# Two transformer blocks: level products of both directions in one, and experts gathered in pairs

## The reference, cut to what matters

```python
b = jnp.cumsum(gc.astype(jnp.float32), axis=2)
diff = jnp.where(lower_tri, b[:, :, :, None, :] - b[:, :, None, :, :], -jnp.inf)
a = jnp.einsum('bhtk,bhsk,bhtsk->bhts', qc, kc, jnp.exp(diff))
o = (jnp.einsum('bhts,bhsv->bhtv', a, vc)
     + jnp.einsum('bhtk,bhkv->bhtv', qc * jnp.exp(b), state))
...
# gla_bidir: for d in range(2), d == 1 with every sequence flipped; the outputs are summed
...
# moe_swiglu
top_v, top_i = lax.top_k(logits, TOP_K)
top_w = jax.nn.softmax(top_v, axis=-1)
gates = jnp.sum(jax.nn.one_hot(top_i, N_EXPERTS, dtype=jnp.float32) * top_w[..., None], axis=-2)
for e in range(N_EXPERTS):
    y = y + gates[..., e:e + 1] * swiglu_2(h, w_gate[e], w_up[e], w_down[e]).astype(jnp.float32)
```

## Time and profile before

| | |
|---|---|
| median of 3 runs | 3079.16 us (3079.08 to 3087.44) |
| the profiled execution | 3083.53 us, of which its span is 3081.6 us |
| mean granted TensorE clock | 0.924 of full speed |
| busy share of the span | TensorE 87%, VectorE 60%, ScalarE 49% |
| bytes read | 558.28 MB, 182 GB/s over the span |
| both level stages | 76.65 us and 45.90 us |
| eight experts | 104.5 us each but the first |

### The profile page before, as it was taken

How to read it: one execution, slowest core, us unless ns; L and a number is a source line. 1 busy time by engine, 2 the same in 40 slices (tenths; PEclk the granted TensorE clock), 3 DMA queues, 4 the chain that set the end, 5 groups by cost and what they waited for, 6 DMA issues and landing times.

```text
span 3081.6 us, 44103 instructions
## 1 busy us (share of the span) xinstructions
PE 2680.0 (87%) x17684; PEld 2350.5 (76%) x17684; DVE 1842.1 (60%) x2603; ACT 1498.9 (49%) x1927; POOL 11.1 (0%) x53
## 2 busy tenths in 40 slices
PE   5987668999989666998878999968899999999997
PEld 3865447999979455997857998947778787878786
DVE  3246734545542564544855554845588888888886
ACT  4224234434442425434454444454467666666665
POOL 0000000000000000000000000000000000000000
PEclk7998878999989877998889999979999999999998
DMA  6250302444533141553412454403388888888884
GB/s 265 83 214 33 137 25 99 178 178 180 187 112 137 69 164 55 179 189 125 151 39 99 151 180 151 177 8 116 116 321 340 323 339 336 332 316 336 337 333 186
DMA packets 80210, 562.10 MB, mean 182 GB/s; under 512 B 8705, under 2 KB 12033, under 8 KB 12434
## 3 DMA queue, kind: packets, MB, share of 16 engines
q1 hardware_dynamic: 79746, 558.32, 48.1%
q0 software_dynamic: 272, 1.05, 0.1%
HBM read 558.28 MB, written 1.05 MB: 182 GB/s over the span
## 4 chain that ended last, share of the span: by engine, by line
PE 77%; DVE 10%; ACT 7%; issue 3%; DMA 0%; DVEq 0%; ACTq 0%; SPq 0%; PEldq 0%; PEld 0%
PE psum L229 76%; ACT ring_hi L220 1%; DVE ring_lo L223 1%; DVE hT L599 1%; DVE Z L1256 1%; DVE hT L372 1%; PE psum L522 1%; ACT hT L358 1%; PE psum L1579 1%; ACT hT L563 1%; DVE Z L1011 1%; DVE Z L1032 1%; ACT a_hi L361 1%; DVE Z L1012 0%; ACT L353 0%
## 5 line engine op out<-in xcount | busy, mean ns | idle before, releaser
L223 DVE TENSOR_TENSOR ring_lo<-ring,ring_hi 128x2048 fp32r<-128x2048 f32 x479 | 1097.1, 2292 | 510.3 <-ACT ring_hi L220 507.4
L220 ACT ACTIVATE ring_hi<-ring 128x2048 fp32r<-128x2048 f32 x479 | 916.0, 1914 | 509.2 <-PE psum L229 508.6
L229 PE MATMUL psum<-a_hi,ring_hi 128*128 128x256 f32 (+1 forms) x2448 | 742.0, 303 | 107.4 <-DVE h_lo L366 50.4
L229 PE MATMUL psum<-a_hi,ring_lo 128*128 128x256 f32 (+1 forms) x2448 | 732.4, 299 | 0.0
L229 PE MATMUL psum<-h_lo,ring_hi 128*128 128x256 f32 (+1 forms) x2128 | 633.8, 298 | 0.0
L229 PEld LDWEIGHTS psum<-a_hi,ring_hi 128*128 128x128 f32 x2448 | 480.5, 196 | 133.4 <-issue 86.7
L229 PE MATMUL psum<-ring_hi,a_hi 128*128 128x512 f32 (+2 forms) x1744 | 538.0, 374 | 6.2 <-DVE h_lo L366 4.0
L229 PEld LDWEIGHTS psum<-a_hi,ring_lo 128*128 128x128 f32 x2448 | 481.8, 197 | 10.4
L229 PEld LDWEIGHTS psum<-h_lo,ring_hi 128*128 128x128 f32 x2128 | 419.7, 197 | 7.5
L229 PE MATMUL psum<-ring_lo,a_hi 128*128 128x512 f32 (+2 forms) x1040 | 371.1, 357 | 0.0
L229 PEld LDWEIGHTS psum<-ring_hi,a_hi 128*128 128x128 f32 x1744 | 325.0, 189 | 58.4 <-issue 4.4
(11 more groups left out here) (222 smaller groups left out, 2529.5 us busy)
## 6 DMA issues: line engine op xcount, KB each, us to landing
ring<-in_stream SPq DMA_DIRECT2D x527, 1024.0 KB, 4.8
cst<-in_constants SPq DMA_DIRECT2D x1, 1216.0 KB
xT<-in_xT SPq DMA_DIRECT2D x1, 1024.0 KB, 9.6
xT<-in_ctxT SPq DMA_DIRECT2D x1, 1024.0 KB, 11.9
xT<-in_memT POOLq DMA_DIRECT2D x1, 1024.0 KB, 8.6
out_y<-hT SPq DMA_DIRECT2D x1, 1024.0 KB, 4.8
Z<-in_level_masks SPq DMA_DIRECT2D x1, 896.0 KB
vec<-in_vectors SPq DMA_DIRECT2D x1, 225.0 KB, 11.0
```

Source lines behind the costliest of these rows:

```text
L220: e.activation(hi, raw, ACT.Copy).then_inc(sem("piece_rounded"), 1)
L223: e.tensor_tensor(lo, raw, hi.bitcast(F32), ALU.subtract).then_inc(sem("piece_split"), 1)
L229: ins = pe.matmul(*args, **kw)
```

## The change

It does four things. (1) One step per level: both directions' decays are formed by instructions over both channel halves (512 columns in layer 0, 256 in layer 1), keys and queries are scaled into two buffers, and one product keys x queries holds one direction above and the other below the diagonal; one mask takes both. Two mod pieces follow a level. VectorE now waits for its own scaling before it overwrites the exponentials. (2) The gather is done for two experts at once: 256 columns in float32r, with the tokens held as a rounded and a rest part (`g_tok`, written by ScalarE and VectorE in the router), so 32 products per pair. Only every second expert has one. (3) The last `turn` of an expert stands behind the first down piece, and the split of one down piece is moved ahead of the last hidden tile on both engines. (4) The scatter is done in two halves, after rounds 2 and 3. The mask table and its load are half as large.

```diff
-            for i, (l, d) in enumerate(gla_steps()):
+            for l in range(LEVELS):
                 await_next(pe, "level")
                 for t in tiles:
                     if t == 3:
-                        pe.wait_ge(sem("gram_read"), rd + (i + 1) * nt + 1)
+                        pe.wait_ge(sem("gram_read"), rd + (l + 1) * nt + 1)
                     else:
-                        pe.wait_ge(sem("gram_read"), rd + i * nt + (nt if t == 0 else t + 1))
+                        pe.wait_ge(sem("gram_read"), rd + l * nt + (nt if t == 0 else t + 1))
                     for h in range(4):
                         r = slice((h % 2) * HD, (h % 2 + 1) * HD)
-                        m = gM[i % 2][r, h // 2, t * P:(t + 1) * P]
-                        mm(pe, gram(t, h), m, m, start=True, stop=True,
+                        at = slice(t * P, (t + 1) * P)
+                        mm(pe, gram(t, h), keys_at[r, h // 2, at], queries_at[r, h // 2, at], start=True, stop=True,
                            last_of="grams" if h == 3 else None)
-                if i < len(IN_LEVELS[layer]):
-                    pe_mod_piece(pe, IN_LEVELS[layer][i])
+                for m in in_level(layer, l):
+                    pe_mod_piece(pe, m)
...
+            def decay(l):
+
                 h = 1 << l
+                for d in range(2):
+                    lo, hi = gla_level(l, gB[d], n)
+                    e_lo, e_hi = gla_level(l, gE[d], n)
+                    m = lo[:, :, :, h - 1:h] if d == 0 else hi[:, :, :, 0:1]
+                    mb = m.to_broadcast([P, 2, n // (2 * h), h])
+                    a, b, ea, eb = (hi, lo, e_hi, e_lo) if d == 0 else (lo, hi, e_lo, e_hi)
+                    dve.tensor_tensor(ea, a, mb, ALU.subtract)
+                    dve.tensor_tensor(eb, mb, b, ALU.subtract).then_inc(sem("level_decay"), 1)
+
+            def scaled(l):
+
+                q, k, keys, queries = (gla_level(l, x, n) for x in (GQ, GK, keys_at, queries_at))
+                e = [gla_level(l, gE[d], n) for d in range(2)]
+                await_next(dve, "level_exp", 2)
+                for half in range(2):
+                    dve.tensor_tensor(keys[half], k[half], e[half][half], ALU.mult)
+                    ins = dve.tensor_tensor(queries[half], q[half], e[1 - half][half], ALU.mult)
                 ins.then_inc(sem("level"), 1)
 
...
-            for i, (l, d) in enumerate(steps):
-                scaled(i)
-                if i + 1 < len(steps):
-                    decay(i + 1)
-                mask = lvl_mask[:, 2 * l + d, :].unsqueeze(1).unsqueeze(1).to_broadcast([P, 2, 2, P])
+            for l in range(LEVELS):
+                scaled(l)
+                await_next(dve, "level")
+                if l + 1 < LEVELS:
+                    decay(l + 1)
+                mask = lvl_mask[:, l, :].unsqueeze(1).unsqueeze(1).to_broadcast([P, 2, 2, P])
                 for t in range(nt):
-                    dve.wait_ge(sem("grams"), gr + nt * (i + 1) + t + 1)
-                    dve.wait_ge(sem("gram_read"), own + nt * i + t + 1)
+                    dve.wait_ge(sem("grams"), gr + nt * (l + 1) + t + 1)
+                    dve.wait_ge(sem("gram_read"), own + nt * l + t + 1)
                     dve.copy_predicated(by_bank(t), mask, grams(t))\
...
-                    dve.tensor_copy(h_tok[:, t, d * 512:(d + 1) * 512], bank[4 + 2 * t + d][:, :])
+                    await_next(dve, "turned_rounded")
+                    at = slice(d * 512, (d + 1) * 512)
...
+            for t in range(2):
+                for d in range(2):
+                    await_next(act, "h_turned")
+                    act.activation(g_tok[t][:, d * 512:(d + 1) * 512], bank[4 + 2 * t + d][:, :], ACT.Copy)\
+                       .then_inc(sem("turned_rounded"), 1)
...
+        def pe_gather(pe, pre, r, pair):
 
             pe.wait_ge(sem(pre + "_selected"), r + 1)
-            for k in range(KT):
+            for k in range(KT if pair else 0):
                 for t in range(2):
-                    mm(pe, bank[6 + k // 4][:, (k % 4) * P:(k % 4 + 1) * P], h_tok[:, t, k * P:(k + 1) * P],
-                       select[:, t, :], start=t == 0, stop=t == 1,
-                       last_of=pre + "_gathered" if k == KT - 1 and t == 1 else None)
+                    mm(pe, g_sums[k // 4][:, k % 4 * T:(k % 4 + 1) * T], g_tok[t][:, k * P:(k + 1) * P],
+                       select[:, t, :, :].rearrange("p u n -> p (u n)"), start=t == 0, stop=False)
+                for t in range(2):
+                    mm(pe, g_sums[k // 4][:, k % 4 * T:(k % 4 + 1) * T], g_tok[2 + t][:, k * P:(k + 1) * P],
+                       select[:, t, :, :].rearrange("p u n -> p (u n)"), start=False, stop=t == 1,
+                       last_of=pre + "_gathered" if k % 4 == 3 and t == 1 else None)
...
+        def act_gather(act, pre, r, i, pair):
+            if pair is not None:
+                for half in range(2):
+                    act.wait_ge(sem(pre + "_gathered"), pair * 2 + half + 1)
+                    act.activation(g_part[0][:, half * 1024:(half + 1) * 1024], g_sums[half], ACT.Copy)\
+                       .then_inc(sem(pre + "_slots_rounded"), 1)
...
+                pos = POS[:, t, following[0]]
+                ins = dve.tensor_scalar(select_w[:, t, :], const("iota"), pos, GT[:, t, following[0]],
                                         ALU.is_equal, ALU.mult)
+                for u in range(2 if pair else 0):
+                    ins = dve.tensor_scalar(select[:, t, u, :], const("iota"), POS[:, t, following[u]], None,
+                                            ALU.is_equal)
...
-                if j == 2:
-                    pe_scatter(pe, pre, r, i)
-            turn(PAIRS - 1)
+                if j in (2, 3):
+                    pe_scatter(pe, pre, r, i, (2 * j - 4, 2 * j - 3))
             for q in range(2 * FT):
...
+                if q == 3:
+                    turn(PAIRS - 1)
                 if q == FT + 1:
                     pe.wait_ge(sem(pre + "_x_added"), r * 4 + 4)
-                    pe_gather(pe, pre, r + 1)
-
-        def act_expert(act, pre, r, i, it):
+                    pe_gather(pe, pre, r + 1, i == 1)
...
+                else:
+                    split_ahead(act, "act", it=it)
...
+                if j in (2, 3):
+                    dve_add_scattered(dve, pre, r, (2 * j - 4, 2 * j - 3))
             for j in range(PAIRS):
-                split_ahead(dve, "dve", it=it)
-                if j == 0:
-                    dve_select(dve, pre, r + 1, following)
-                if j == PAIRS // 2 + 1:
-                    dve_gather(dve, pre, r + 1)
+                if j:
+                    split_ahead(dve, "dve", it=it)
+                else:
+                    dve_select(dve, pre, following, i == 1)
+                if j == PAIRS // 2 + 1 and i == 1:
+                    dve_gather(dve, pre, pair + 1)
```

More of the change, by code:

```diff
@@ L932, in by_bank, with in_level @@
             return gA[:, t].rearrange("p (v u) n -> p u v n", v=2)
-        def gla_steps():
-            return [(l, d) for l in range(LEVELS) for d in range(2)]
+        def in_level(layer, l):
+            return IN_LEVELS[layer][2 * l:2 * l + 2]
         def pe_gla_levels(pe, layer):
@@ L969, in act_gla_levels @@
             n = 2 * T if layer == 0 else T
[L970 to L977, removed]
+            for l in range(LEVELS):
+                for d in range(2):
+                    await_next(act, "level_decay")
+                    e = gE[d][:, :, 0:n]
+                    act.activation(e, e, ACT.Exp).then_inc(sem("level_exp"), 1)
+                for m in in_level(layer, l - 1) if l else ():
+                    act_mod_rows(act, m, batch(layer)[0], rows_a)
+            for m in in_level(layer, LEVELS - 1):
+                act_mod_rows(act, m, batch(layer)[0], rows_a)
             phase_end(act)
@@ L982, in dve_gla_levels @@
             nt = n // P
-            steps = gla_steps()
-            def decay(i):
-                l, d = steps[i]
+            def decay(l):
                 h = 1 << l
[L989 to L992, removed]
-                    mb = m[:, c].to_broadcast([P, n // (2 * h), h])
-                    a, b = (hi, lo) if d == 0 else (lo, hi)
-                    ea, eb = (e_hi, e_lo) if d == 0 else (e_lo, e_hi)
-                    dve.tensor_tensor(ea[:, c], a[:, c], mb, ALU.subtract)
-                    ins = dve.tensor_tensor(eb[:, c], mb, b[:, c], ALU.subtract)
-                ins.then_inc(sem("level_decay"), 1)
@@ L1518, in build, with pe_scatter @@
         PAIRS = FT // 2
-        def pe_scatter(pe, pre, s, i):
+        def pe_scatter(pe, pre, s, i, blocks):
             pe.wait_ge(sem(pre + "_y_copied"), s * 2 + 2)
-            for b in range(4):
+            for b in blocks:
                 if b >= 2:
@@ L1529, in pe_scatter, with dve_add_scattered @@
                        start=True, stop=True, last_of=pre + "_scattered" if c == 1 else None)
```

(21 more changed lines are left out.)

90 lines of the change are left out of this document (35 added, 55 removed).

## The result

The changed kernel takes 2992.22 us, the median of four runs (2987.19 to 2995.16), against 3079.62 for the kernel before in the same session (four runs). The ratio is 0.971, with a 95% interval from 0.969 to 0.973: 87 us faster, where 70 were forecast. The profiled execution took 2990.49 us, 93.0 less than that of before.

The account below looks back on a forecast made before the run. VectorE was taken to bound the levels and TensorE the experts. Levels and mask cast 32.8 us plus experts 37.2 made 70.0 saved, from a median of 3079.2 to 3009 us; own range 2999 to 3024, wide range 2992 to 3038.

Parts of the forecast that it names:

- The scatter: In each expert, TensorE's 1.21 us idle mid-scatter would vanish with two blocks in each of two rounds: 9.7 us saved.
- The turning: Before each expert's last hidden-tile turning, TensorE's 2.01 us idle would be filled by four down blocks: 16.1 us saved.
- The gather: Token gather for two experts at once, 32 float32r products of 256 columns in 3.84 us: 13.4 us saved in the loop.
- the late split: Behind the last turning, the fourth down piece's split comes some 0.3 us late in every second expert: 1.2 us lost.
- The levels: Merged level steps: 7.4 us per level in layer 0, 4.1 in layer 1; 19.9 and 12.4 us saved.
- the 0.3 taken off for TensorE's start: Layer 1's levels: 0.3 us deducted from 12.7 saved, because TensorE's first products came at half speed.
- The columns: Modulation columns behind the levels in both layers: no saving in the main forecast, 0 us.
- The transfers bind: Experts' pieces come no faster than 336 GB/s, so only the levels pay: 3046 us; chance 0.06.
- The clock falls in the levels: TensorE, less busy in the level stages, loses clock: price 10 to 19 us, 3019 to 3028; chance 0.12.
- Its opposite: TensorE's clock stays up for the 48 records behind the levels in both layers: 8 us more gained, 3001; chance 0.1.
- The split pieces come late: At four reordered expert places TensorE waits for VectorE's splits: 18 us each per expert; chance 0.07 one or two, 0.03 four.
- The change does nothing: Across the whole kernel, what is removed was already hidden, so the time stays 3079 us; chance 0.02.

Follow-up runs that it names:

- the changed kernel's repeat: The changed kernel timed again without any edit, in the third experiment session beside three variants: 2993.07 us, 0.971 of the kernel before.

## Why the prediction was right or wrong

The mechanisms were right, each where it was said to be. The saving was mis-sized by 17 to 23 us, in these terms.

**The scatter: 1.21 us forecast per expert, 1.67 measured.** The bracket is only the idle time of the one wait; start to start the scatter went from 4.75 to 3.08 us (16 records of 0.19). 8 times the difference is 3.7 us; putting the scatter back costs 12.9 in all.

**The turning: 2.01 forecast, 2.24 measured**, for the same reason: the wait has 0.2 us of its own around the bracket. 1.8 us.

**The gather was right.** 3.84 us per pair as forecast, against 2 x 3.57, or 13.2 us for four pairs, with 12.7 measured alone. So was the late split: in the second expert of a pair VectorE's six comparisons put the split of the fourth down piece so that one product begins 0.44 us after another instead of 0.23: 0.2 us late, where the forecast had 0.3. TensorE, there, in the changed kernel:

```profile
2541.66 0.39 PE L229 MATMUL psum<-ring_lo,Zr 128*128 128x512 f32 x1
2542.10 0.72 PE L229 MATMUL psum<-ring_hi,Zr 128*128 128x512 f32 x2
```

Experts in one sum: 17.9 (turning), 13.3 (scatter), 13.2 (gather), 8.0 (clock) are 52.4; products that take 91.6 us per expert instead of 91.2 in one without a fall give back 3. Half of that is a price of the second scatter round that the forecast didn't have: the product behind a round takes 0.42 us instead of 0.23, start to start. The late split is 0.1 per expert. The profile says 49.4.

**The levels: 32.3 us forecast, 36.0 profiled.** Periods of 7.40 and 4.05 us were forecast as 7.4 and 4.1. In layer 0 VectorE's busy time fell by 20.9, 1 us more than seven times the period's saving. In layer 1 the 0.3 taken off for TensorE's start didn't come: VectorE's idle time in the stage fell from 2.98 to 1.30 us.

**The columns: 0 forecast, 5.9 profiled, of which only some 3 belong to the change.** The wait behind unchanged levels was 9.60, 9.60, 9.60, 6.80, 6.80 and 6.67 us in layer 0 in six profiled executions, and 11.6 to 13.0 in layer 1; behind merged levels 4.97, 4.98, 6.18, 6.52, 6.80 and 7.08 in six (the seventh, with split instructions, had 9.60), and 10.5 to 11.2. The means differ by 2.1 and 1.3. The profiled execution of before was on the high side in both. The difference is the granted clock, 0.50 and 0.90 in the groups of layer 0 of the kernel before and of the changed kernel's repeat:

```profile
361.60:372.00 10.40, 10.40 (x50) 10.31 (x48) 0.73 (x1) 0.00 (x0) 0.00 (x0) 0.50 0.00 0
339.77:345.83 6.06, 6.06 (x50) 5.98 (x48) 1.13 (x2) 0.00 (x0) 0.00 (x0) 0.90 0.44 170
```

That the columns' time turns on the clock was said; that it differs by 3 us between executions of equal work was not.

**Rivals.** *The transfers bind*: false. The three whole pairs drew 352 to 353 GB/s, more than the 336 that an expert had shown, and no wait for a transfer stands in them. By the 358 GB/s per core of the Trainium skill (DMA: Bandwidth & Descriptors, Where 436 GB/s comes from) a pair of two times 33 pieces could not be under some 193 us, an estimate; 196.8 us come near that and decide nothing about it. *The clock falls in the levels*: it was 0.91 in layer 0, down from 0.96, and 0.89 again in layer 1, but the periods stood at VectorE's time, so in the levels themselves it cost nothing that shows. *Its opposite*, columns at full clock with 8 us more: half right in the profile, 3 us by all executions. *The split pieces come late*: only as forecast, 0.2 us a pair. The turning moved without its splits shows that this rival had a real price, all of the turning's gain. *The change does nothing*: false.

## What to carry to other kernels

An idle time on TensorE is worth more than its bracket: measure it start to start, and look whether the products behind it run at half clock, in every repetition of the loop and not in one, since only some showed it here. When a step moves past another, what other engines do ahead for it has to move too, or the wait reappears at the next product with nothing gained. Work which nobody waits for until the end of a stage (columns here) is cheaper in that stage's gaps, as long as it stands behind, not in front of, the products that the bounding engine needs.

## What the runs showed of the hardware that was not expected

Useless products made a kernel faster: eight per expert, in an idle time of 2.0 us, saved 7.5 us of 3084 (95% interval 4 to 11). A float32r product of 128 columns costs nearly what one of 256 does (0.11 against 0.120 us), one of 512 costs 0.227. Products with two columns take as long as their weights' loads, 7.27 us for 48 records whose loads are busy for 7.2: start to start 0.112 us each at full clock and 0.213 at half. The 64 of layer 1 took 11.6 us in the changed kernel, and VectorE waited 10.5 for them. And programs whose work is equal up to some place reached it 3.6 us apart (layer 0's first decay at 285.4 and 289.0 us in two profiled executions), with a mean clock of 0.79 and 0.72 from 250 to 282 us.
